# VectorE's order at the end of the first even head, rearranged around the two rotations

## The reference

```
def even_layer(x, norm_w, w_in, w_out, lam_p, lam_init, subln_w, hg_norm_w, lb, cos, sin):
    h = rmsnorm(x, norm_w)
    proj = jnp.einsum('bsd,de->bse', h, w_in)
    qa, ka, va, ga, qh, ffw, fbw, ih, gh = split_cols(proj, EVEN_SIZES)
    oa = differential_attention(qa, ka, va, lam_p, lam_init, subln_w, cos, sin) * jax.nn.silu(ga)
    ob = hgrn2_bidirectional(qh, ffw, fbw, ih, lb, hg_norm_w) * jax.nn.silu(gh)
    return jnp.einsum('bse,ed->bsd', jnp.concatenate([oa, ob], axis=-1), w_out)
```

## Time and profile before

| | |
|---|---|
| median of 3 runs | 1157.49 us (1157.34, 1157.49, 1159.63) |
| profiled execution: its own time / its span | 1158.41 us / 1156.6 us |
| TensorE busy | 1127.6 us (97%) |
| VectorE busy | 977.4 us (85%) |
| ScalarE busy | 677.1 us (59%) |
| mean granted TensorE clock | 0.997 |

### The profile page before, as it was taken

The page is one execution under the profiler, slowest core; times in us unless marked ns, Lnnn a source line. Parts: engine busy times, 40 slices in busy tenths (PEclk is TensorE's granted clock), DMA queues, the critical chain, the costliest instruction groups (busy, mean ns, idle before and its releaser), DMA issues. The chain is left out here.

```text
span 1156.6 us, 18631 instructions
## 1 busy us (share of the span) xinstructions
PE 1127.6 (97%) x5750; PEld 913.4 (79%) x5750; DVE 977.4 (85%) x1927; ACT 677.1 (59%) x1324; POOL 0.2 (0%) x4
## 2 busy tenths in 40 slices
PE   6999999999999999999999999999999999999996
PEld 5877778778778778778778877887888888888875
DVE  6879889889889889789789898888888888888886
ACT  6474564564564564564654674366666666666654
POOL 0000000000000000000000000000000000000000
PEclk9999999999999999999999999999999999999999
DMA  7613422522422423323324220554232324323112
GB/s 211 158 56 92 138 64 56 145 65 58 130 73 61 121 73 75 107 73 86 96 73 98 85 73 19 124 137 122 80 91 54 91 66 120 101 59 91 55 38 73
DMA packets 131817, 103.60 MB, mean 90 GB/s; under 512 B 5440, under 2 KB 116416, under 8 KB 131776
## 3 DMA queue, kind: packets, MB, share of 16 engines
q1 hardware_dynamic: 131776, 103.07, 32.7%
HBM read 77.88 MB, written 2.10 MB: 69 GB/s over the span
## 5 line engine op out<-in xcount | busy, mean ns | idle before, releaser
L74 PE MATMUL bank_proj<-hH,w_hi 128*128 128x512 f32 x856 | 343.1, 401 | 1.3 <-issue 1.2
L76 PE MATMUL bank_proj<-hH,w_lo 128*128 128x512 f32 x856 | 334.5, 391 | 0.0
L75 PE MATMUL bank_proj<-hL,w_hi 128*128 128x512 f32 x856 | 334.3, 391 | 0.0
L76 PEld LDWEIGHTS bank_proj<-hH,w_lo 128*128 128x128 f32 x856 | 160.8, 188 | 35.2
L74 PEld LDWEIGHTS bank_proj<-hH,w_hi 128*128 128x128 f32 x856 | 161.5, 189 | 32.8 <-issue 1.9
L75 PEld LDWEIGHTS bank_proj<-hL,w_hi 128*128 128x128 f32 x856 | 161.4, 189 | 30.9 <-issue 0.5
L1943 ACT ACTIVATE probs<-bank_odd_score,small 128x256 f32<-128x256 f32 (+1 forms) x128 | 66.3, 525 | 73.9 <-DVE small L2181 73.9
L1220 DVE TENSOR_TENSOR w_lo<-w_raw,w_hi 128x1024 fp32r<-128x1024 f32 x74 | 89.4, 1217 | 9.3 <-ACT w_hi L710 9.3
L710 ACT ACTIVATE w_hi<-w_raw 128x1024 fp32r<-128x1024 f32 x74 | 78.0, 1055 | 28.9 <-DMA w_raw<-in_w_in_even 28.4
L1950 ACT ACTIVATE probsT<-bank_odd_turn 128x256 fp32r<-128x256 f32 (+1 forms) x128 | 49.0, 434 | 61.8 <-PE bank_odd_turn L1677 61.7
L775 ACT ACTIVATE probs<-bank_score,small 128x512 f32<-128x512 f32 x64 | 43.4, 684 | 60.0 <-DVE small L1058 53.2
(11 more groups left out here) (412 smaller groups left out, 2219.0 us busy)
## 6 DMA issues: line engine op xcount, KB each, us to landing
w_raw<-in_w_in_even SPq DMA_DIRECT2D x72, 512.0 KB, 4.9
w_raw<-in_w_in_odd SPq DMA_DIRECT2D x36, 512.0 KB, 4.4
qs<-parts SPq DMA_DIRECT2D x96, 128.0 KB, 2.3
ks<-parts SPq DMA_DIRECT2D x40, 256.0 KB, 4.4
o_raw<-in_w_out_even SPq DMA_DIRECT2D x15, 512.0 KB, 6.2
o_raw<-in_w_out_odd SPq DMA_DIRECT2D x14, 512.0 KB, 6.7
out<-w_raw SPq DMA_DIRECT2D x8, 256.0 KB, 2.1
mixT<-in_x SPq DMA_DIRECT2D x2, 512.0 KB, 5.4
```

What stands on the lines that cost most here:

```text
L74: pe.matmul(out, hi, moving_hi, start=start, stop=False)
L75: pe.matmul(out, hi, moving_lo, start=False, stop=False)
L76: return pe.matmul(out, lo, moving_hi, start=False, stop=stop)
```

## The change

In the first head alone, VectorE's calls after `normalize(h, 0)` are put in another order. `gate_and_split(h, 0)` goes to the very end of the head, and `place_level`, `near_scale` and `scale_vt` calls go ahead of the rotation next to them. No instruction is added or removed, and the other engines' programs are as before.

```diff
--- before.py
+++ after.py
@@ -1343,27 +1343,44 @@
                     low_out(h, 0)
                     low(h, 9)
                 normalize(h, 0)
-                gate_and_split(h, 0)
+                if not first:
+                    gate_and_split(h, 0)
                 near_scale(h, 2)
                 near_differences(h, 4)
                 near_scale(h, 3)
                 near_differences(h, 5)
-                rotate(h, 7)
-                low(h, 10)
-                near_scale(h, 4)
-                near_differences(h, 6)
-                place_level(h, 2)
-                near_scale(h, 5)
-                place_level(h, 3)
-                low(h, 11)
-                rotate(h, 8)
-                scale_vt(h, 9, 2)
-                place_level(h, 4)
-                near_scale(h, 6)
+                if first:
+                    place_level(h, 2)
+                    near_scale(h, 4)
+                    near_differences(h, 6)
+                    low(h, 10)
+                    rotate(h, 7)
+                    place_level(h, 3)
+                    near_scale(h, 5)
+                    low(h, 11)
+                    scale_vt(h, 9, 2)
+                    place_level(h, 4)
+                    near_scale(h, 6)
+                    rotate(h, 8)
+                else:
+                    rotate(h, 7)
+                    low(h, 10)
+                    near_scale(h, 4)
+                    near_differences(h, 6)
+                    place_level(h, 2)
+                    near_scale(h, 5)
+                    place_level(h, 3)
+                    low(h, 11)
+                    rotate(h, 8)
+                    scale_vt(h, 9, 2)
+                    place_level(h, 4)
+                    near_scale(h, 6)
                 scale(h, 10, keys[:, 0])
                 place_level(h, 5)
                 place_level(h, 6)
                 low_out(h, 1)
+                if first:
+                    gate_and_split(h, 0)
 
             def end_of_last(h):
                 place_diagonal(h)
```

## The result

The change comes out at 1160.34 us (median of 20 runs, 1157.24 to 1162.25), against 1157.78 us for the kernel before (20 runs, 1156.38 to 1159.63). The ratio is 1.0017 with an interval of 1.0011 to 1.0024: slower by about 2.0 us by the ratio and by 2.56 us between the medians. The ratio is inside the 0.2% that I called no change, though its interval lies wholly on the slow side and reaches past 0.2%.

The account below looks back on a forecast made before the run. TensorE, busy nearly throughout, was taken as the bound, with a DMA-fed chain limiting its lead. 4.23 us gained, 1.2 and 2.6 lost to waits, 1.63 to the clock: +1.2 on 1157.49 gives 1158.7 us, range 1155.6 to 1160.4.

Parts of the forecast that it names:

- The wait at level 4: First head: TensorE's 2.44 us wait for VectorE's level 2 copy goes; with its slow clock, 4.23 us given back.
- The term that the change adds: End of first head: second rotation starts 1.22 us later, at 109.0, and so do the key moves and loads behind it.
- The landing: Loads behind the key moves: if the first and third share bandwidth, the first lands up to 0.6 us later still.
- A new wait of 1.2 us: Second head's `scores`: TensorE arrives at 120.3 us, but the last key move lands only at 121.5.
- The squares: L491, sum of squares: TensorE waits 2.6 us for the late low part, up to 130.9, leaving it 0.4 us early.
- The clock: Behind the 2.6 us wait at the squares: TensorE's clock falls as it did at level 4, costing 1.63 us.
- The sum: Whole kernel: −0.4 us of lead left at the squares plus 1.63 us of slow clock makes +1.2 us.
- rival (c): Clock falls at the squares' new wait but had not fallen at level 4 before: 2.8 us slower, 1160.3; chance 0.15.

Follow-up runs that it names:

- e1: The changed kernel with the first head's second rotation put back ahead of the values' scaling, level 4's copy and level 6's scaling: 1158.76 us, ratio 1.0004.
- e6: The changed kernel with attention's gate and split back in its old place, so only the new order remains: 1160.53 us, ratio 1.0020.
- e4: The changed kernel with 14 unread matmuls in TensorE's order ahead of head 1's wait for the squares' low part: 1159.12 us, ratio 1.0008.
- e7: The kernel of e2 with the gate and split put off into head 1, level 2's copy before level 6's differences, projection 4's load before the key moves: 1152.95 us.
- e2: The kernel before with attention's gate and split moved to the first head's end as the only edit: 1155.26 us, ratio 0.9980.
- e3: The changed kernel with the load of the next head's projection 4 ahead of the first head's key moves on SyncE: 1157.35 us, ratio 0.9995.
- e5: The kernel before with 10 unread matmuls ahead of level 4 in the first head: 1156.80 us, ratio 0.9992.

## Why the prediction was right, and where not

**The wait at level 4** went for the reason given, with every start within half a microsecond: level 2's copy at 96.65 (forecast 96.8), the first rotation at 100.74 (100.93), projection 2 at 111.18 (111.67), clock 1.00.

**The term that the change adds**, 1.22 us later for the second rotation and all that hangs on it, held: 108.81 (109.0; 1.03 later than before, and 1.21 when the 0.18 us by which this execution runs ahead is added), keys 112.82 (113.0), loads 116.40 (116.6), L710 at 122.86 (123.1). e1 and e6 move the rotation the other way and by more, and L710 follows each time.

**The landing** took 6.46 us from issue to L710 (before 6.48), though the third load was in flight beside the first for longer. The 0.6 us that I allowed for sharing, for which I had shown no working, were not there. That agrees with what the Trainium skill, "DMA: Bandwidth & Descriptors", section "Queues, rings and completion order", says: each DMA engine consumes the descriptors of a ring in their order. That a later load therefore can't slow an earlier one was my conclusion, and it rests on this one pair.

**The step that failed** is "A new wait of 1.2 us" at `scores`. I had taken the slowest landing of one execution, 6.7 us, for the last key move; it was 5.0 us this time, as in seven of the nine profiles of this document, and TensorE passed `scores` with no wait. The total did not suffer, since the wait only moved on: 3.89 us at L491, for 1.2 + 2.6 = 3.8 forecast. A chain that ends later than another hides an error in the other.

**The squares** are at 130.62 (130.9), so the lead was eaten as worked out. **The clock** fell where I had taken it from one earlier case: 1.75 us for 1.63, and e4 shows that it does not come when the idle time is filled. The transpose of `vt` is 1.09 us late for a forecast of 1.2.

**The sum** was 1.2, and 2.0 was measured by the ratio, 2.56 between the medians. The median of 1160.34 lies 1.64 us above the forecast's 1158.7: 0.29 is the base, 1157.78 in twenty runs where three had given 1157.49, and the rest is the size. Rival (c) had put it at 1160.3. That the wide range still holds the median, by 0.06 us, is luck.

In the profiled executions the surplus is not in the first head at all: the 1.09 us of lateness there, close to the forecast, have shrunk to 0.5 by the last odd layer, where I had let all of it reach the end, and the clock falls once more there, behind a wait that both kernels have. So two errors worked against each other: lateness that is lost on the way, and a fall that the sum does not have. That fall comes in a part of the executions. In the nine profiles (both kernels and e1 to e7) the clock fell at this place in after, e1 and e4, and not in the other six.

The mean granted clock of the single executions says more. The profile before, with one fall, has 0.997; those of e2 and e7, with none while TensorE works, have 0.999. Of the 54 executions of the kernel before that were run beside e1 to e7, five have 0.999 and took 1156.49 to 1157.16 us: it does not always pay the fall at level 4. At the other end five of the 20 of the changed kernel and five of the 11 of e6 have 0.993 or 0.994 and took 1160.36 to 1162.25 us, and none of the 54 has less than 0.995, the 21 on e6's own chip among them. So the new order meets more slow clock in a part of its executions, and that is what rival (c) built on, with its 2.8 us for rarer falls before and surer falls after. How often, and at which places, is open: none of those ten executions was profiled, and the mean also takes in the end of the span, where TensorE has no work left and the clock falls in every profile. The gap that the first 20 executions of the kernel before leave between 1157.93 and 1158.86 us says nothing, since the 54 others fill it.

**What I did not ask** is whether the two halves of the change have opposite signs. They have: the split's move alone is 0.998, the order alone 1.002. The split's move removes most of the wait and makes the keys earlier; the order removes the rest of the wait, 0.76 us, and makes the keys 2.7 us later (110.16 in e2, 112.82 in the change). The two do not add up: 0.998 and 1.002 would make 1.000, and the change has 1.0017. In the new order level 2's copy has to wait for TensorE (0.81 us idle ahead of 96.65), so the split's move brings the second rotation only 0.71 us earlier (109.52 in e6, 108.81 in the change) and the squares 0.43.

## What to carry to other kernels

A wait that goes is worth what the next meeting of the two engines lets through: before counting it, walk to that meeting and compare both arrivals, as here 1.7 us to spare at the squares against 4.2 gained. In this kernel it paid that work which feeds a DMA and a chain behind it (rotation, keys, loads, weights, softmax, squares) goes ahead of work that feeds only this head's own matmuls, as long as those are not late by more than a fraction of a microsecond (0.24 and 0.55 us in e7, against 1.82 in e1); and a result that nobody needs for long (here `y`) is the first thing to put off. When a change is made of several moves, time them apart, since a gain and a loss can lie under one small number.

## What the runs showed of the hardware

Behind idle times of TensorE of 2.27, 2.44, 3.89 and 4.00 us (e3, before, after, e6; one profile each) its clock fell to 0.50 for about 3 us, and behind two waits of 1.82 and 0.56 us as well (e1). Behind one of 1.59 us near the end it stayed at 1.00 in six of nine profiles and fell in three, with the same instructions around it. Each fall cost 1.3 to 1.8 us. With matmuls that nobody reads issued into the wait it stayed at 1.00 (e4, e5; one profile each).

The four moves of the keys, 256 KB each within SBUF, landed 3.0 to 6.7 us after their issue in two of the nine profiles (before, e7) and 3.0 to 5.0 in the other seven. e5, where SyncE and VectorE have the order of before, is one of the seven: the slowest landing of one execution is not a duration to build on to a microsecond.
